# Seven modulation blocks of layer 1: rows weighted and summed on VectorE, TensorE summing over partitions once per unit

## What is computed

```
silu_c  = silu(c)            # (1, 1024), latents
silu_cc = silu(c_ctx)        # (1024,),   context
for l in range(2):
    mod_lat = split(silu_c  @ w_ada[l] + b_ada[l], 6)     # w_ada[l]: 1024 x 6144
    mod_ctx = split(silu_cc @ w_ada[l] + b_ada[l], 6)
    ...
    f = silu(h @ ffn_w_gate) * (h @ ffn_w_up)             # layer 0: 512 tokens, 1024 -> 2816
    ... f @ ffn_w_down
```

## Time and profile before

| | before |
|---|---|
| median of 3 runs | 1668.63 us (1667.31 to 1669.69) |
| the profiled execution | 1667.8 us |
| its span, first to last instruction | 1666.1 us |
| TensorE busy | 1591.3 us, 96% |
| VectorE busy | 703.0 us, 42% |
| ScalarE busy | 375.8 us, 23% |
| GpSimd busy | 80.5 us, 5% |
| granted TensorE clock, mean | 0.991 |
| gate and up stage on TensorE | 345.4 to 624 us of the span |

### The profile page before, as it was taken

One profiled execution on the slowest core, in us unless ns is written; L12 is line 12 of the kernel. 1 busy time (PEld: TensorE's weight loads), 2 busy tenths in 40 slices (PEclk: granted clock), 3 DMA queues, 4 the chain that ended last, 5 costly groups with the idle time before them and its releaser, 6 DMA issues.

```text
span 1666.1 us, 26910 instructions
## 1 busy us (share of the span) xinstructions
PE 1591.3 (96%) x11354; PEld 963.6 (58%) x11354; DVE 703.0 (42%) x1657; ACT 375.8 (23%) x841; POOL 80.5 (5%) x156
## 2 busy tenths in 40 slices
PE   6999999989999999999898999899999999999997
PEld 3655456868888888885676545334344443334344
DVE  4987983574544456877589360000010001000101
ACT  4333543321111010015756522100000000000002
POOL 2210100000000003000003100000000000000000
PEclk9999999999999999999999999999999999999999
DMA  8503553235536515204144389999999999999995
GB/s 320 168 8 121 208 147 101 85 116 153 152 108 195 148 42 127 89 3 150 57 125 112 92 344 388 413 415 407 407 412 414 408 405 411 414 409 406 411 412 211
DMA packets 170839, 396.41 MB, mean 238 GB/s; under 512 B 34499, under 2 KB 93483, under 8 KB 153562
## 3 DMA queue, kind: packets, MB, share of 16 engines
q1 hardware_dynamic: 165344, 391.23, 63.6%
q0 software_dynamic: 4112, 3.34, 1.3%
q10 hardware_dynamic: 1258, 0.07, 0.0%
HBM read 389.36 MB, written 1.05 MB: 234 GB/s over the span
## 4 chain that ended last, share of the span: by engine, by line
PE 82%; DMA 8%; DVE 5%; ACT 2%; SPq 1%; issue 1%; ACTq 0%; DVEq 0%
PE ps L1362 80%; DMA arena<-in_moe_w_up_dram 4%; PE ps L1365 2%; DMA arena<-in_moe_w_down_dram 2%; DMA arena<-in_w_in_dram 1%; DMA arena<-in_moe_w_gate_dram 1%; SPq L705 1%; DVE arena L2743 1%; ACT work L866 0%; ACT work L865 0%; DVE work L2418 0%; DVE work L2420 0%; DVE work L2423 0%; DVE norms L2421 0%; DVE norms L2569 0%
## 5 line engine op out<-in xcount | busy, mean ns | idle before, releaser
L1362 PE MATMUL ps<-arena,work 128*32 128x256 f32 (+6 forms) x4572 | 605.5, 480 | 13.9 <-DMA arena<-in_moe_w_up_dram 7.7
L1362 PEld LDWEIGHTS ps<-arena,work 128*32 128x32 f32 (+2 forms) x4572 | 271.4, 125 | 318.4 <-issue 249.3
L1362 PE MATMUL ps<-arena 128*128 128x256 f32 (+2 forms) x1152 | 289.7, 479 | 5.7 <-DMA arena<-in_w_in_dram 4.7
L1362 PEld LDWEIGHTS ps<-arena 128*128 128x128 f32 (+1 forms) x1152 | 185.9, 185 | 99.6 <-issue 72.3
L1362 PE MATMUL ps<-work 128*64 128x64 f32 (+11 forms) x2300 | 222.1, 323 | 12.7 <-DVE work L2991 6.7
L3222 DVE TENSOR_TENSOR work<-work,ps 128x768 f32<-128x768 f32 (+4 forms) x26 | 18.6, 726 | 510.4 <-PE ps L1362 510.4
L1362 PEld LDWEIGHTS ps<-work 128*64 128x64 f32 (+5 forms) x2300 | 156.2, 150 | 71.3 <-issue 53.6
L1362 PE MATMUL ps<-work,arena 128*128 128x256 f32 (+1 forms) x588 | 126.5, 367 | 0.0
L1282 ACT ACTIVATE work<-ps 128x512 f32<-128x512 f32 (+3 forms) x35 | 17.7, 505 | 444.8 <-PE ps L1365 444.8
L1362 PEld LDWEIGHTS ps<-work,arena 128*128 128x128 f32 (+1 forms) x588 | 103.2, 190 | 13.4
L1362 PE MATMUL ps<-apad,dg 64*64 64x512 f32 (+1 forms) x384 | 69.2, 500 | 9.0 <-ACT dg L874 5.9
(11 more groups left out here) (438 smaller groups left out, 1392.8 us busy)
## 6 DMA issues: line engine op xcount, KB each, us to landing
arena<-in_moe_w_down_dram SPq DMA_DIRECT2D x66, 1024.0 KB, 17.2
arena<-in_moe_w_up_dram SPq DMA_DIRECT2D x54, 1024.0 KB, 18.4
arena<-in_w_ada_dram SPq DMA_DIRECT2D x23, 2048.0 KB
arena<-in_moe_w_gate_dram SPq DMA_DIRECT2D x46, 1024.0 KB, 15.8
arena<-in_moe_w_up_dram SPq DMA_DIRECT2D x26, 768.0 KB, 16.9
arena<-in_moe_w_gate_dram SPq DMA_DIRECT2D x22, 768.0 KB, 15.8
norms<-in_moe_w_down_dram SPq DMA_DIRECT2D x13, 1024.0 KB, 16.8
arena<-in_w_in_dram SPq DMA_DIRECT2D x6, 2048.0 KB
```

The lines of the kernel that those rows point to most:

```text
L1362: return pe.matmul(o, lhs, rhs, start=start, stop=stop)
```

## The change

Seven blocks, 1 to 3 of unit (1, 0) and 0 to 3 of unit (1, 1), are no longer multiplied by TensorE block by block. VectorE takes them (`weigh`): each of the 1024-row unit's row blocks is multiplied by its per-partition condition value and added up, for each of the two streams, into `mod_sum[s]` (128 x 2048; stream 0 in `spare`, stream 1 in the interior of `apad`). A block is 16 pieces (`PIECES`) of 128x512: 2 row blocks x 2 streams x 4 quarters. The eight pieces of a unit's first row block are a `tensor_scalar`, all others a `scalar_tensor_tensor` with its scalar from `sc`. The pieces are spread over both steps of stage i = 1, 2, 3, 5, 6, 7, 8: two and three in the step j = 0, then four, two, two and three in the step j = 1. A counter `ada_part` rises with each piece, and a piece waits for the one eight before it.

TensorE then sums over partitions once per unit: `summed_modulation` is 2 streams x 4 column groups of matmuls with a 128x32 matrix that has ones in one column (`one_at`). It runs after step 8 for unit (1, 0), on top of block 0 in bank 7, and after step 18 for unit (1, 1). `modulate(1, 0)` moves from step 8 to step 10, `modulate(1, 1)` from 18 to 20.

The ring's order becomes A0 F0 F1 A1 F2 A2 F3 A3 F4 F5 A5 F6 A6 F7 A7 F8 A8 F9 F10, with Ai now the block that VectorE uses in stage i, and the slot of such a block is released by `ada_part`, at VectorE's 16th piece.

```diff
+        one_at = view(4096, [33], "x")
+        PIECES = 16
+        SUMMED = {i: (1, 0, i) for i in range(1, BLOCKS)}
+        SUMMED.update({SECOND + b: (1, 1, b) for b in range(BLOCKS)})
+        summed_before = lambda i: PIECES * sum(1 for x in SUMMED if x < i)
+        mod_sum = (spare[:, 1152:1152 + NU].rearrange("p (a i t) -> p a i t", a=4, i=2), inner)
...
-            used.append(("ada_done", BLOCKS * UNITS.index((l, u)) + b + 1))
+            summed = [i for i in SUMMED if SUMMED[i] == (l, u, b)]
+            used.append(("ada_part", summed_before(summed[0] + 1)) if summed else
+                        ("ada_done", BLOCKS * UNITS.index((l, u)) + b + 1))
...
+                add_block(*UNITS[3], 0)
                 for i in range(FU):
-                    if i < BLOCKS:
-                        add_block(*UNITS[3], i)
-                    if SECOND <= i < SECOND + BLOCKS:
-                        add_block(*UNITS[4], i - SECOND)
+                    if i - 1 in SUMMED:
+                        add_block(*SUMMED[i - 1])
...
+            def summed_modulation(bank, blocks, count):
+                pe.wait_ge(sem("ada_part"), summed_before(blocks[-1] + 1))
+                for s in range(2):
+                    v = mod_sum[s].rearrange("p a i (m j r) -> p j (a i) m r", j=4, r=32)
+                    for j in range(4):
+                        last = mm(ps[32 * j:32 * j + 32, bank, :], one_at[:, 1 - s:33 - s], v[:, j],
+                                  count == BLOCKS and s == 0, s == 1)
+                last.then_inc(sem("ada_done"), count)
...
-                    if j and i < BLOCKS - 1:
-                        modulation(at["ada", 1, 0, i + 1], i + 1, 7)
-                    if j and SECOND <= i + 1 < SECOND + BLOCKS:
-                        if i + 1 == SECOND:
-                            pe.wait_ge(sem("mod"), 4)
-                        modulation(at["ada", 1, 1, i + 1 - SECOND], i + 1 - SECOND, 7)
+                    if b == 2 * BLOCKS:
+                        summed_modulation(7, range(1, BLOCKS), BLOCKS - 1)
+                    if b == 2 * (SECOND + BLOCKS):
+                        pe.wait_ge(sem("mod"), 4)
+                        summed_modulation(7, range(SECOND, SECOND + BLOCKS), BLOCKS)
...
+                    def weigh(i, first, last):
+                        l, u, blk = SUMMED[i]
+                        n, before_ = at["ada", l, u, blk], summed_before(i)
+                        if first == 0:
+                            dve.wait_ge(sem(f"ring_in{n % 3}"), landed[n])
...
+                        for x in range(first, last):
+                            k, s, q = x // 8, x // 4 % 2, x % 4
+                            o = mod_sum[s][:, q]
+                            w = weights(n)[:, k, 512 * q:512 * q + 512].rearrange("p (i t) -> p i t", i=2)
+                            c_k = sc[:, 2 * blk + k, s:s + 1]
+                            if k == 0 and i in (1, SECOND):
+                                ts_(o, w, c_k, None, ALU.mult).then_inc(sem("ada_part"), 1)
+                            else:
+                                dve.wait_ge(sem("ada_part"), before_ + x - 7)
+                                stt(o, w, c_k, o, ALU.mult, ALU.add).then_inc(sem("ada_part"), 1)
...
                         combine(b, c11, product(2), sum1, product_of=2)
+                        if full_part:
+                            weigh(i, 5, 9)
                         combine(b, sum1, product(6), sum1, after=1, product_of=6)
+                        if full_part:
+                            weigh(i, 9, 11)
                         dve.wait_ge(sem("ffn_t"), 2 * b + 2)
                         combine(b, c12, product(3), p5, product_of=3)
                         combine(b, c12, c12, sum1, after=3)
+                        if late_part:
+                            weigh(i, 0, 2)
+                        if full_part:
+                            weigh(i, 11, 13)
                         combine(b, sum1, product(7), sum1, after=4, product_of=7)
...
+                        if late_part:
+                            weigh(i, 2, 5)
+                        if full_part:
+                            weigh(i, 13, PIECES)
```

More of the change, by code:

```diff
@@ L2998, in _ @@
                     tt_(T_of(4), second[0], T_of(2), ALU.subtract).then_inc(sem("ffn_tokens"), 1)
+                    def weigh(i, first, last):
[3 more added lines that the diff above has]
+                            dve.wait_ge(sem(f"ring_in{n % 3}"), landed[n])
+                            if i == 1:
+                                link(dve.memset(one_at, 0.0))
+                                link(dve.memset(one_at[:, 1:2], 1.0))
+                            if i == SECOND:
+                                dve.wait_ge(sem("ada_done"), BLOCKS * (UNITS.index((1, 0)) + 1))
+                        for x in range(first, last):
[8 more added lines that the diff above has]
+                                stt(o, w, c_k, o, ALU.mult, ALU.add).then_inc(sem("ada_part"), 1)
                     for b in range(2 * FU):
                         i, j = b // 2, b % 2
+                        late_part = j == 0 and i in SUMMED
+                        full_part = j == 1 and i in SUMMED
                         if b + 1 < 2 * FU:
@@ L3007, in _ @@
                             seventh_sums(0, 0)
-                        if b == 2 * BLOCKS:
+                        if b == 2 * BLOCKS + 2:
                             modulate(1, 0, 7, rowsT)
-                        if b == 2 * (SECOND + BLOCKS):
+                        if b == 2 * (SECOND + BLOCKS) + 2:
                             modulate(1, 1, 7, rowsT)
```

## The result

| | before | after |
|---|---|---|
| median of 6 runs | 1668.46 us (1667.31 to 1669.69) | 1658.28 us (1657.30 to 1659.68) |
| ratio of the runs | | 0.9939, 95% interval 0.9929 to 0.9949 |
| the profiled execution, its span | 1667.8, 1666.1 us | 1659.7, 1657.9 us |
| VectorE busy | 703.0 us | 769.3 us |
| instructions on TensorE | 11354 | 11274 |

The kernel is 10.2 us faster. The forecast was 9.25 us and 1659.4. The forecast time was 1.1 us too high, and the measured one lies inside the forecast case's own range. The page of after, sections 1 and 4, answers to the earlier trace rows; by the first line TensorE lost 80 records, five groups of sixteen, and 11.2 us of busy time, and VectorE gained 66 us.

The account below looks back on a forecast made before the run. TensorE's instructions, end to end in the gate and up stage, were taken as the bound: -12.95 us for seven blocks plus 3.70 for two summed ones gave -9.25 us, median 1668.63 to 1659.4, range 1657.2 to 1662.8.

Parts of the forecast that it names:

- the forecast case: Whole kernel: 9.25 us saved, median 1659.4 us, own range 1657.4 to 1661.8, chance 0.78.
- Where the time went: Gate and up stage: TensorE's instructions lie end to end for 303.08 us, so time taken from them leaves the span.
- The price of a group: Gate and up stage on TensorE: each modulation block takes 1.85 us, seven removed give 12.95 us.
- The summed group's price: Two summed modulations on TensorE: 1.85 us each, 3.70 in all; at most 2.4 us each, 1.1 more for both.
- VectorE's cost: VectorE in the gate and up stage: 71 us of new pieces, lying beside TensorE at no price.
- The layout in time: A full stage: VectorE runs some 5 us late without growing later, and waits some 1 us for the ffn tile.
- the rule of the Trainium skill: VectorE: next operation waits for the pipe to empty; as whole lengths, 24.8 us per 24.17 us stage, 0.6 later each.
- The slack: Bank of product 2 in a stage's second step: wanted at 13.8 us, freed at 7.9, so 5.9 us to spare.
- (2): Full stages: VectorE needs 26.5 to 27 us and gives 2 to 6 us back, 1661.5 to 1665.2; chance 0.10.
- (4): Ring cycle bounds the seven stages; slower than before above 27.2 us a stage, 0.95 a piece; 1678 at 28.5; chance 0.05.
- The sum of rival (4): Seven stages: lost time is 7(X - 24.17) minus 11.8 us, X being VectorE's time a stage; 18.5 us at 28.5.
- (3): Experts at the end: TensorE arrives 9 us early and waits for weights, losing the gain; 1665.3 to 1669; chance 0.07.

Follow-up runs that it names:

- apart5: The changed kernel plus five groups of 128x32 zero matmuls on TensorE, after steps 1, 3, 5, 11 and 13: 1669.08 us, 1.0001 to before.
- dose_a: The changed kernel plus an unused 128x128 VectorE addition ahead of each of the 112 pieces: 1657.86 us, 0.9932 to before.
- dose_b: The changed kernel plus an unused 128x288 VectorE addition ahead of each of the 112 pieces: 1670.13 us, 1.0010 to before.
- dose_c: The changed kernel plus an unused 128x416 VectorE addition ahead of each of the 112 pieces: 1684.69 us, 1.0096 to before.
- together5: The changed kernel plus five zero-matmul groups, two back to back with the first summed group and three with the second: 1666.87 us, 0.9989 to before.

## Why the prediction was right, and what was off

**Where the time went** held: a stage that is TensorE's alone, and the gain is five groups fewer (apart5 brings the time back to 1.0001).

**The price of a group** is the term that was mis-sized, 1.85 us where it is 2.06. I took the distance from the group's first record to the next product's. The stage's period was in the same rows: 370.04 to 396.27 is 26.23 us, and a stage without a group 24.17, so 2.06. Most of the difference of 0.21 lies on both sides: the product ahead hands over some 0.1 us later (its last eight records start at 366.37, and the group at 368.19 rather than 1.73 later), and the product behind takes 3.72 instead of 3.62 us for sixteen records. The summed group costs the same: 439.09 to 465.34 is 26.25, 2.08 more than two plain steps. The sum becomes -7 x 2.06 + 2 x 2.08 = -10.3 us, against 10.2 in the medians and 10.20 in the last column of the table.

**The summed group's price** was bounded above by 2.4 us for another source of the operand. `spare` and the gapped `apad` take 1.07 us each for eight records in the timeline, alike. The bound was not needed.

**VectorE's cost** held: the rows of after give 34.3 + 33.8 us for 96 `scalar_tensor_tensor`, 0.71 by merged length and 0.66 start to start, and a `tensor_scalar` in 0.48 where 0.50 was estimated, so some 70 us for the 71 forecast. (VectorE's busy time, which counts overlapping instructions once, rose by 66.3.)

```profile
L3035 DVE SCALAR_TENSOR_TENSOR arena<-arena,sc 128x512 f32<-128x512 f32 x48 | 34.3, 744 | 0.0
L3035 DVE SCALAR_TENSOR_TENSOR apad<-arena,sc,apad 128x512 f32<-128x512 f32 x48 | 33.8, 747 | 0.0
L3032 DVE TENSOR_SCALAR arena<-arena,sc 128x512 f32<-128x512 f32 x8 | 3.5, 480 | 0.0
L3032 DVE TENSOR_SCALAR apad<-arena,sc 128x512 f32<-128x512 f32 x8 | 3.5, 481 | 0.0
```

**The layout in time** held: 5.1 us of lateness forecast, 5.3 to 5.8 where it has settled, with one of 6.3; a wait of 1 us for the tile, 1.09 and 1.37 measured in the first unit and 2.01 once in the second. The instructions of VectorE start 0.60 to 0.67 apart with lengths of 0.69 and 0.75, so the rule of the Trainium skill (VectorE: DVE Perf Modes, "The DRAIN you can't avoid"), taken as whole lengths, does not hold between independent ones here either. The prediction left out that the same section adds that a next instruction that is not held starts earlier, and with that the trace agrees. dose_a adds 3.1 us to a full stage (16 of 112 additions, 21.7 us in all), where whole lengths would have added 2.1, and costs nothing.

**The slack** of 5.9 us held. dose_a is 2 to 4 us later than the changed kernel and free; in dose_b TensorE first waits, 0.77 us, at 11.7 us of lateness, which puts the limit at 10.9 us, against 5.1 + 5.9 = 11.0. The bank of product 2 in the second step was also the place forecast.

**The rivals.** (2) and (4) were one mechanism at two sizes, and it exists: its price came out at 26.4 us for dose_c. Rival (4) put the point from which the kernel is slower than before at 0.95 us a piece. Measured, 0.86 is free and 1.03 gives 1.0010, so it lies between; by the one for one of the larger doses it is at some 1.02 (estimated). The sum of rival (4), seven stages over 24.17 less the slack used twice, was too steep: it gives 18.5 us of lost time for a piece of 1.03 (X of 28.5), and 11.8 were lost. It would have been better to take it from the layout than from a sum over seven stages, since a unit's first stage has cheap pieces and starts without lateness: the layout for a piece of 1.03 gave 10 us, and 11.8 came. (3), a gain that is lost later, is not seen: the stage from product 3 on gives 10.2 us in both profiles, the medians 10.2 and 10.3.

## What to carry to other kernels

When one engine's instructions fill a stage end to end, price a removed group by the period of stages with and without it, not by its own records: the neighbours change too. When work goes to an engine beside it, lay one period out in time with the arrivals that it waits for, and look for the first buffer whose release comes too late; the sum of busy time says neither that 93% of the period (22.5 of 24.17 us) is harmless, nor that the same work placed at the end of the period costs all of the gain. If that engine also releases a slot of a weight ring, its lateness comes back to it as a late load, so release early rather than last. And a wait of the filled engine can cost more than its length: behind the 6.7 us before step 0, and behind waits of 3 us in dose_c, TensorE ran for a few us at half its clock.

## What was new about the hardware

Two shapes of matmul next to each other cost something. A group of sixteen 128x32 records costs 1.72 us behind another such group and 2.06 between products of 128x128. In the timeline of the weight loads of before, the load for the first 128x128 matmul behind a group starts only at 396.26, when the group's matmuls end (394.41 + 1.92), 0.84 us after the last load; within a product the loads follow each other without a gap. Between two groups back to back in together5 the loads are 0.30 us apart, and 0.87 behind the last of them.

```profile
395.30 0.13 PEld L1362 LDWEIGHTS ps<-arena,sc 128*32 128x32 f32 x4 [0.30 <-issue]
396.26 3.32 PEld L1362 LDWEIGHTS ps<-arena 128*128 128x128 f32 x16 [0.84 <-issue]
```

That this missing overlap is what the 0.34 us are is what the rows suggest; no run here changed the shapes to test it.
